# Down phase of a Strassen-like MLP: four products share one PSUM accumulation and go straight to the residual

## The reference, cut to what matters

```
h = rmsnorm(x, p['norm_mlp'][layer])
x = x + (jnp.square(jax.nn.relu(h @ p['mlp_up'][layer])) @ p['mlp_down'][layer]).astype(dt)
```

## Time and profile before

| | us |
|---|---|
| median of 3 runs | 3397.2 |
| the profiled execution | 3398.76, its span 3397.0 |
| PE busy | 3205.9 (94%) |
| DVE busy | 2139.8 (63%) |
| POOL busy | 1336.3 (39%) |
| ACT busy | 1166.3 (34%) |
| down phase of layer 0, first to last matmul's start | 1641.14 to 2000.31 |
| down phase of layer 1 | 3027.57 to 3380.39 |

### The profile page before, as it was taken

How to read it: one execution, slowest core, us unless ns; L and a number is a source line. 1 busy time by engine, 2 the same in 40 slices (tenths; PEclk the granted TensorE clock), 3 DMA queues, 4 the chain that set the end, 5 groups by cost and what they waited for, 6 DMA issues and landing times. The chain is left out here.

```text
span 3397.0 us, 74922 instructions
## 1 busy us (share of the span) xinstructions
PE 3205.9 (94%) x31716; PEld 3028.7 (89%) x31716; DVE 2139.8 (63%) x2868; ACT 1166.3 (34%) x2373; POOL 1336.3 (39%) x792
## 2 busy tenths in 40 slices
PE   7999889999998998999899979999998899989996
PEld 7998768888887888999899879999998899989996
DVE  5112874764665658666666874566546966666678
ACT  3344122333333334444333332221222444433333
POOL 3322120110113035444777843222212544467774
PEclk9999889999999999999999989999999999999998
DMA  5113630010011112444644311111112244454442
GB/s 169 57 57 107 190 118 12 26 36 15 23 36 53 60 48 86 140 143 143 212 140 145 90 38 57 59 65 63 58 68 102 67 147 142 140 187 143 140 140 77
DMA packets 151199, 322.70 MB, mean 95 GB/s; under 512 B 16904, under 2 KB 50356, under 8 KB 150744
## 3 DMA queue, kind: packets, MB, share of 16 engines
q1 hardware_dynamic: 106480, 242.53, 22.1%
q10 hardware_dynamic: 44392, 75.42, 6.5%
HBM read 227.12 MB, written 93.12 MB: 94 GB/s over the span
## 5 line engine op out<-in xcount | busy, mean ns | idle before, releaser
L247 PE MATMUL psum<-act_hi,w_hi 128*128 128x352 f32 x2088 | 706.9, 339 | 29.4 <-DVE act_lo L353 14.9
L232 POOL TENSOR_TENSOR w_hi<-w_raw,derived 128x1024 fp32r<-128x1024 f32 x87 | 171.2, 1968 | 1428.1 <-PE psum L247 1346.3
L247 PE MATMUL psum<-act_hi,w_lo 128*128 128x352 f32 x2088 | 679.5, 325 | 0.0
L247 PE MATMUL psum<-act_lo,w_hi 128*128 128x352 f32 x2088 | 678.8, 325 | 0.0
L247 PEld LDWEIGHTS psum<-act_hi,w_hi 128*128 128x128 f32 x2088 | 399.0, 191 | 58.2 <-issue 24.5
L247 PEld LDWEIGHTS psum<-act_lo,w_hi 128*128 128x128 f32 x2088 | 400.3, 192 | 2.5 <-issue 0.2
L247 PEld LDWEIGHTS psum<-act_hi,w_lo 128*128 128x128 f32 x2088 | 399.7, 191 | 0.0
L1019 PE MATMUL psum<-ff_near,ff_w_hi 128*128 128x264 f32 x2048 | 381.5, 287 | 9.0 <-ACT ff_a L1147 5.9
L1019 PEld LDWEIGHTS psum<-ff_near,ff_w_hi 128*128 128x128 f32 x2048 | 318.7, 189 | 15.5 <-issue 15.0
L1019 PE MATMUL psum<-ff_far,ff_w_hi 128*128 128x264 f32 x1536 | 289.8, 289 | 20.4 <-ACT ff_c L1147 10.7
L1019 PE MATMUL psum<-ff_near,ff_w_lo 128*128 128x264 f32 x1024 | 291.8, 285 | 0.0
(11 more groups left out here) (552 smaller groups left out, 7506.8 us busy)
## 6 DMA issues: line engine op xcount, KB each, us to landing
ff_du_raw<-u SPq DMA_DIRECT2D x224, 264.0 KB, 2.8
w_raw<-weights SPq DMA_DIRECT2D x87, 512.0 KB, 3.3
u<-ff_stage SPq DMA_DIRECT2D x128, 264.0 KB, 2.1
ff_raw<-mlp SPq DMA_DIRECT2D x64, 512.0 KB, 3.9
u<-ff_side SPq DMA_DIRECT2D x96, 264.0 KB, 3.6
s_cache<-cache_a ACTq DMA_DIRECT2D x32, 512.0 KB, 6.8
...
```

The lines of the kernel that those rows point to most:

```text
L232: pool.tensor_tensor(hi, raw, self.zeros, ALU.add).then_inc(s.sem, s.step())
L247: last = pe.matmul(out, w[:, k, :], h[:, k, cols], start=(start and k == ks[0] and m == 0), stop=(stop and k == ks[-1] and m == 2))
```

## The change

It changes the order of products, where their results go, and who makes which weight sum. Nothing in the up phase changes but the order in its last pair.

- `ORDER` becomes `DOWN`: groups 0 to 2 run products 2, 4, 1, 6, 7, 5, 3, the last group 4, 1, 6, 7, 5 and then 2, 3 in the half units. Products 6, 7 and 5 (`CHAINED`) do not clear their banks: they accumulate onto 1, onto 1+6 and onto 1+6+7.
- After each step DVE adds what the banks hold to x at once (`targets`): one add for products 1, 2, 3, 4 and 6, two for 7 and 5 (with a subtraction that takes 1+6+7 out of one quadrant again). The `ff_sum` tiles, `spread` and `corner` are gone.
- The weight sums move: in group 0, `side_sum` stands after step 1's low parts and `column_sum` is done by DVE after step 0; in later groups they stand in the last step of the group before and the first of their own. `corner_sum` and `row_sum` follow products 1 and 6 wherever these stand.
- The tiles `one` and `two` change places in SBUF, and so SP's order of loads: the tiles of product 2 and 4 come first. In the last pair of the up phase ACT copies `ff_c` ahead of the activations' high parts, and DVE makes the fourth quadrant ahead of their low parts.

```diff
-    ORDER = (1, 6, 5, 7, 4, 2, 3)
...
+    DOWN = ((2, 4, 1, 6, 7, 5, 3),) * (GROUPS - 1) + ((4, 1, 6, 7, 5, 2, 3),)
+    CHAINED = (6, 7, 5)
     UNITS = (3, 1, 0, 2)
-    KEPT = (1, 5, 6, 7)
...
-        if p in self.KEPT:
-            t = self.sum_of[p, d]
-            return t[:, :, :] if tp is None else t[:, tp]
-        return self.tokens(d + (4 if p == 4 else 0), 1 if p == 3 else 0, tp)
+    def targets(self, p, d):
+
+        return {1: ((d, 0, ALU.add),), 2: ((d, 0, ALU.add),), 3: ((d, 1, ALU.add),), 4: ((4 + d, 0, ALU.add),),
+                6: ((d, 1, ALU.add),), 7: ((4 + d, 0, ALU.add), (d, 1, ALU.subtract)),
+                5: ((4 + d, 1, ALU.add), (d, 1, ALU.add))}[p]
...
@@ -962,37 +956,22 @@
             for p in (1, 2, 6, 7, 5, 3, 4):
                 self.weight_low(pool, w, p)
         four = range(self.WIDTH)
-        self.w_lower(pool, 0, 0)
-        for q in (0, 1):
-            self.side_sum(pool, s, 0, q)
-        self.w_lower(pool, 0, 1)
-        for q in (0, 1):
-            self.column_sum(pool, s, 0, q)
-        for q in (2, 3):
-            self.w_lower(pool, 0, q)
-        for q in (2, 3):
-            self.side_sum(pool, s, 0, q)
-        for q in (2, 3):
-            self.column_sum(pool, s, 0, q)
         for step in range(self.STEPS):
             g, m = divmod(step, 7)
-            if step:
+            for q in four:
+                self.w_lower(pool, step, q)
+            if step == 1 or m == 6 and g + 1 < self.GROUPS:
                 for q in four:
-                    self.w_lower(pool, step, q)
-            if m == 0:
+                    self.side_sum(pool, s, 0 if step == 1 else g + 1, q)
+            if g and m == 0:
+                for q in four:
+                    self.column_sum(pool, s, g, q)
+            if self.product_of(step) == 1:
                 for q in four:
                     self.corner_sum(pool, g, q)
-            if m == 1:
+            if self.product_of(step) == 6:
                 for q in four:
                     self.row_sum(pool, g, q)
-            if m == 5 and g + 1 < self.GROUPS:
-                for q in four:
-                    self.side_sum(pool, s, g + 1, q)
-                for q in four:
-                    self.column_sum(pool, s, g + 1, q)
-            if g == self.GROUPS - 1 and 3 <= m < 6:
-                for d in self.UNITS:
-                    self.corner(pool, (6, 5, 7)[m - 3], d)
 
 
     def pe(self, pe):
...
         out = K.psum[:, bank, 0:HC]
+        fresh = self.product_of(step) not in self.CHAINED
         for q in range(self.WIDTH):
             if first:
                 pe.wait_ge(*at(f"split.{n}.W{step}.{q}"))
@@ -1053,7 +1033,8 @@
             w_hi, w_lo = self.w_place(step, q)
             u_hi, u_lo = self.u_place(step, q)
             for m, (w, u) in enumerate(((w_hi, u_hi), (w_hi, u_lo), (w_lo, u_hi))):
-                last = pe.matmul(out, w[:, d], u[:, tp], start=(q == 0 and m == 0), stop=(q == self.WIDTH - 1 and m == 2))
+                last = pe.matmul(out, w[:, d], u[:, tp], start=(fresh and q == 0 and m == 0),
+                                 stop=(q == self.WIDTH - 1 and m == 2), skip_group_check=True)
...
         self.w_high(act, 0, 1)
         keep_both(w, 1)
+        self.w_high(act, 0, 2)
+        keep_both(w, 2)
         for q in range(self.WIDTH):
             self.u_high(act, 0, q)
-        self.w_high(act, 0, 2)
-        keep_both(w, 2)
         self.w_high(act, 0, 3)
         self.square_out(act, w, "22")
```

The adds of DVE, before and after:

```diff
-        p, src = self.product_of(step), K.psum[:, 2 * d:2 * d + 2, 0:HC]
-        dst = self.target(p, d)
+        src = K.psum[:, 2 * d:2 * d + 2, 0:HC]
         dve.wait_ge(*at(f"pe.{n}.D{step}.{d}"))
-        if step == 0 and d == self.UNITS[0]:
-            dve.wait_ge(K.plan.dve_done, K.plan.before(f"dve.{n}.D0.{d}"))
-            dve.wait_ge(*at(f"act.{n}.{self.PAIRS - 1}.sq21"))
-        if step < 7 and p == 5:
-            for m in (1, 2, 3, 7):
-                dve.wait_ge(K.sem(f"{n}_u{m}_stored"), 16 * self.PAIRS)
-        if step >= 7:
-            dve.wait_ge(*at(f"dve.{n}.x21.7.{d}" if step == self.STEPS - 3 else f"dve.{n}.D{step - 7}.{d}"))
-        if step < 7 and p in self.KEPT:
-            dve.tensor_copy(dst, src).then_inc(s.sem, s.step(f"dve.{n}.D{step}.{d}"))
-        else:
-            dve.tensor_tensor(dst, dst, src, ALU.add).then_inc(s.sem, s.step(f"dve.{n}.D{step}.{d}"))
-
-    def spread(self, dve, p, d):
+        if step:
+            dve.wait_ge(*at(f"dve.{n}.D{step - 1}.{d}"))
+        targets = self.targets(self.product_of(step), d)
+        for k, half, op in targets:
+            dst = self.tokens(k, half)
+            label = "D" if (k, half, op) == targets[-1] else "E"
+            dve.tensor_tensor(dst, dst, src, op).then_inc(s.sem, s.step(f"dve.{n}.{label}{step}.{d}"))
+
...
-        dst = self.target(p, d, tp)
+        dst = self.tokens(d, half, tp)
         dve.tensor_tensor(dst, dst, self.K.psum[:, u % self.RING, 0:HC], ALU.add).then_inc(s.sem, s.step(f"dve.{n}.F{u}"))
...
         w = self.PAIRS - 1
         self.quadrant(dve, w, "11")
+        self.quadrant(dve, w, "22")
         for q in range(self.WIDTH):
             self.u_lower(dve, 0, q)
-        self.quadrant(dve, w, "22")
         self.quadrant(dve, w, "12")
+        self.quadrant(dve, w, "21")
         self.mixed_out(dve, w)
-        self.quadrant(dve, w, "21")
         self.mixed_last(dve, w)
-        last = self.STEPS - 7
         for step in range(self.STEPS - 2):
-            g, m = divmod(step, 7)
             for j, d in enumerate(self.UNITS):
                 self.down_add(dve, step, d)
-                if step >= last:
-                    self.spread(dve, self.product_of(step), d)
                 if j < 2:
                     for q in (2 * j, 2 * j + 1):
                         self.u_lower(dve, step + 1, q)
+            if step == 0:
+                for q in range(self.WIDTH):
+                    self.column_sum(dve, s, 0, q)
```

SP's loads ahead of the down phase:

```diff
             else:
-                one(0, 0)
-                one(0, 1)
+                for half in range(2):
+                    two(0, 0, half)
+                    two(0, 1, half)
             for p in (5, 7, 6, 2):
                 store(w, p)
         store(end - 1, 4)
         for q in (2, 3):
+            two(0, q, 0)
+        for q in range(self.WIDTH):
+            u_load(0, q)
+        for q in (2, 3):
+            two(0, q, 1)
+        for q in range(self.WIDTH):
+            u_load(1, q)
+        for q in range(self.WIDTH):
             one(0, q)
-        for q in (0, 1):
-            two(0, q, 1)
-        for s in range(2):
-            for q in range(self.WIDTH):
-                u_load(s, q)
-        for q in (0, 1):
-            two(0, q, 0)
-        store(end, 1)
-        for half in (1, 0):
-            for q in (2, 3):
-                two(0, q, half)
-        for p in (3, 5, 7, 6, 2, 4):
+        for p in (1, 3, 5, 7, 6, 2, 4):
             store(end, p)
```

More of the change, by code:

```diff
@@ L595, in down_places @@
         block = lambda b: W_HI + b * W_TILE
-        u_at = lambda s, q: F + (4 * q + 2) * WIDE if s == 0 else G + ((4, 7, 2, 5), (0, 3, 6, 1))[s % 2][q] * WIDE
+        u_at = {"first": [F + (4 * q + 2) * WIDE for q in range(4)], "even": [G + n * WIDE for n in (4, 7, 2, 5)],
+                "odd": [G + n * WIDE for n in (0, 3, 6, 1)]}
         raw_at = LEFT + 32 * P + WIDE
@@ L600, in down_places @@
                 (block(0), block(3), rstd_at, G + 14 * WIDE),
-                (raw_at, raw_at + W_TILE, G + 15 * WIDE, G + 13 * WIDE))
+                (F + 6 * WIDE, G + 13 * WIDE, G + 15 * WIDE, F + 15 * WIDE))
         self.u_op, self.w_op = {}, {}
-        for which, s in (("first", 0), ("even", 2), ("odd", 1)):
+        for which, places in u_at.items():
             for q in range(self.WIDTH):
-                self.u_op[which, q] = tuple(K.at(f"{name}_du_{which}{q}_{part}", [P, 2, HC], F32R, u_at(s, q) + n * half)
+                self.u_op[which, q] = tuple(K.at(f"{name}_du_{which}{q}_{part}", [P, 2, HC], F32R, places[q] + n * half)
                                             for n, part in enumerate(("hi", "lo")))
@@ L719, in one, with two @@
             if g:
-                sp.wait_ge(*at(f"split.{n}.W{7 * g - 4}.{q}"))
+                sp.wait_ge(*at(f"split.{n}.S4_{g - 1}.{q}"))
+                sp.wait_ge(*at(self.split_of(7, g - 1, q)))
+            else:
+                sp.wait_ge(*at(f"pe.{n}.{end}.P{1 if q < 2 else 7}.1"))
+            sp.dma_start(self.one[q][:, :], tile(g, q, 0)).then_inc(K.sem(f"{n}_one{q}"), 16)
+        def two(g, q, half):
+            if g and half:
+                sp.wait_ge(*at(f"split.{n}.S1_{g - 1}.{q}"))
+                sp.wait_ge(*at(self.split_of(4, g - 1, q)))
+            elif g:
                 sp.wait_ge(*at(f"split.{n}.S4_{g - 1}.{q}"))
@@ L728, in one @@
                 sp.wait_ge(*at(f"pe.{n}.{end}.P1.1"))
```

(18 more changed lines are left out.)

74 lines of the change are left out of this document (22 added, 52 removed).

## The result

The changed kernel takes 3356.9 us, median of 4 runs (3353.18 to 3362.83); the kernel before, on the same chip, 3397.1 (3390.91 to 3401.65). The ratio is 0.9884, 95% interval [0.9863, 0.9906]: 1.2% faster. A second set gave 3360.7 against 3396.2, ratio 0.989 [0.9873, 0.9908]. 3355 was forecast, in a range of 3341 to 3374.

A forecast was written before the change was run, and what follows sets the result against it. TensorE keeps pace in the middle; 69.8 us is lost at starts and ends of both down phases. Gains 9.5 + 8.4 + 0.7 + 0.7 + 12.6 + 9.9 = 41.8 us off 3398.8: 3357.0, forecast as 3355 (3341 to 3374).

The forecast's parts named there:

- The start: Up phase's last three products and down phase's first steps: 4.5 us still lost per layer, gaining 9.5 and 8.4.
- V4's wait: DVE's last operand sum before the down phase: waits for a store, priced at 3.05 us from the pair before.
- step 1's fourth low part: Low parts DVE makes for the down phase's step 1: late, stalling PE by 2.6 us.
- The wait for `ff_b`: Up phase's last pair: SP's four smaller loads delay PE through `ff_b` by 0.7 us, bounds 0 and 3.
- The sums are gone from their way: Down phase's step 1: its weights' low parts no longer stand behind POOL's twelve sums.
- The middle: Steps 2 to 23: DVE keeps pace despite double adds; 0.4 us lost, 0.7 gained in each layer.
- D: Steps 24 and 25: DVE's and POOL's extra adds go; 0.5 us lost where 13.1 and 13.2 were.
- E: Closing units: the chain through the norm's square stays, losing 10.4 us in layer 0 and 6.8 in layer 1.
- the start gains little: Rival, 15%: S3 and the store hold DVE back, PE waits in steps 1 and 2; gain 24, time 3373.
- better than that: Rival, 22%: DVE keeps up in steps 1 and 2, `ff_b` delay nil; gain 52, time 3345.
- Slower by double adds: Rival, 4%: DVE's double adds bound products 7 and 5, 16 steps losing 3.0 us each; time 3403.
- D's stalls are not DVE's: Rival, 4%: activation loads or POOL's lower weights are late in steps 24 and 25; gain 29, time 3368.

The follow-up runs named there:

- second profile: The changed kernel unaltered, profiled and timed once more against the kernel before: 3360.7 us, ratio 0.989.
- experiments 5 and 6: 5: changed kernel with V4 after step 0's adds, its store after step 2's activation loads, 3360.2 us; 6: also S3 later, 3351.1 us.
- experiment 8: Changed kernel with V4 and S3 later, and SP issuing the second halves of the first four `two` tiles behind the first halves: 3356.1 us.
- experiments 1 and 4: 1: kernel before with only the last pair's new order, 3402.5 us; 4: changed kernel with the last pair's old order, 3374.9 us.
- experiment 3: Changed kernel with a third PSUM add in each unit of products 7 and 5: 3366.6 us.
- experiment 2: Kernel before without POOL's `corner` adds to x in the last group and the waits for them: 3383.4 us.
- experiment 7: Changed kernel with the norm's sums of the first three closing units behind the last low part on DVE: 3356.5 us.

## Why the prediction was right, and where its terms were off

The sign, the places and the time were right. The sum forecast 28.0 us left of what the MLPs lost; 33.6 and 35.2 were. So 41.8 us of gain were forecast and the two MLPs gained 36.7 and 35.1. The two medians nevertheless lay within 2 to 6 us of 3355, because the rest of the program varies by as much: part of that closeness is luck.

- **The start, 4.5 us forecast in each layer, 7.8 and 6.9 measured (7.7 and 9.2 in the second profile).** This is the step that was mis-sized. The order of what is late was right (DVE: V4, S3, low parts; experiments 5 and 6 show both). Wrong was the price of V4's wait. It was read from the pair before, 3.05 us; in the last pair DVE comes to V4 sooner than before, while the store that frees its buffer stands behind the loads and takes 6.0 us, and V4 waited 4.76. That is 1.7 us, and it made step 1's fourth low part not 2.6 but 4.3 us late. (The prediction's own numbers, 3.5 us less 1.1, give 2.4 and not 2.6.) Then 3.4 us at half clock followed, some 1.7 us, which stood only in the bound. Step 2 lost 0.6 of the 1.2 forecast. The wait for `ff_b` cost 1.3 and 1.5 instead of 0.7; experiment 8 shows that it was the loads' order, as the prediction said.
- **"The sums are gone from their way"** was right, and needed both parts of the change (experiments 1 and 4). That the change of order alone gives nothing was not in the prediction.
- **The middle, 0.4 forecast, 0.2 measured** (with step 2 apart). The PSUM adds took 687 to 706 ns in all 272 cases; experiment 3 shows that even a third of them per unit costs 1 us in a layer.
- **D, 0.5 forecast, 0 measured.** The cause given, DVE and POOL in each other's way, is shown by experiment 2. By the change D gains 13.1 and 13.2.
- **E, 10.4 and 6.8 forecast, 10.4 and 8.0 measured.** Layer 1 lost its cover as said; the slow stretch that comes with the wait was 6.8 us at half clock, 3.4 us, and had been put at 1. Experiment 7 shows that the chain through the norm's square costs 5.5 of the 8.0 us in layer 1; in layer 0 it shows only 2.9 of the 10.4, as another wait takes its place.

Of the rivals, "the start gains little" and "better than that" each hold a little: V4 and S3 do hold DVE back, and without them the start is free. "Slower by double adds" and "D's stalls are not DVE's" have fallen.
